# A trunk layer with 32 experts: the order of the last experts' weights, the selection tables and the final store are rearranged

## What is computed

```python
def hier_moe(h, lp):                      # top-1 of 4 groups, top-2 of 8 experts in it
    ...
    for e in range(N_EXPERTS):            # 32 experts, D 1024, D_EXPERT 256
        hid = jax.nn.silu(t @ lp['exp_w_gate'][e]) * (t @ lp['exp_w_up'][e])
        y = y + comb[:, e:e + 1] * (hid @ lp['exp_w_down'][e])
...
x = ln_affine(DEEPNORM_ALPHA * x + g2 * hier_moe(h2, lp), lp['ln2_g'], lp['ln2_b'])
```

## Time and profile before

| | us |
|---|---|
| time, median of 3 (715.06 to 717.89) | 716.77 |
| the profiled execution | 715.41 |
| its span in the trace | 713.7 |
| TensorE matmul busy | 635.1 (89%) |
| VectorE busy | 277.9 (39%) |
| ScalarE busy | 109.6 (15%) |
| GpSimd busy | 113.1 (16%) |

### The profile page before, as it was taken

The page is one execution under the profiler, slowest core; times in us unless marked ns, Lnnn a source line. Parts: engine busy times, 40 slices in busy tenths (PEclk is TensorE's granted clock), DMA queues, the critical chain, the costliest instruction groups (busy, mean ns, idle before and its releaser), DMA issues.

```text
span 713.7 us, 8198 instructions
## 1 busy us (share of the span) xinstructions
PE 635.1 (89%) x3225; PEld 346.4 (49%) x3225; DVE 277.9 (39%) x568; ACT 109.6 (15%) x227; POOL 113.1 (16%) x115
## 2 busy tenths in 40 slices
PE   2899999999999999999999974899998888888894
PEld 0374345554444455556444453566664544544431
DVE  2421543236745445213224766133333222322247
ACT  0020252220012122215010020211111001100000
POOL 3000000020300000000000221433333222231100
PEclk9679999999999999999999985799999999999998
DMA  9977444236430230308968087599999999999852
GB/s 337 368 247 252 161 182 149 87 118 236 141 119 5 113 118 1 118 3 298 370 246 321 29 296 292 190 406 405 406 405 405 407 404 403 400 403 402 353 214 88
DMA packets 67495, 176.60 MB, mean 247 GB/s; under 512 B 10420, under 2 KB 12500, under 8 KB 67456
## 3 DMA queue, kind: packets, MB, share of 16 engines
q1 hardware_dynamic: 50832, 143.56, 52.8%
q10 hardware_dynamic: 10880, 24.21, 9.6%
q0 software_dynamic: 5744, 8.28, 3.3%
HBM read 174.55 MB, written 11.96 MB: 261 GB/s over the span
## 4 chain that ended last, share of the span: by engine, by line
PE 69%; DMA 15%; DVE 6%; SPq 6%; issue 2%; ACT 1%; POOL 1%; DVEq 0%; POOLq 0%
PE bank L1478 24%; PE bank L1733 10%; DMA X<-exp_w_up 9%; PE bank L1650 6%; PE bank L1664 6%; PE bank L1742 5%; DMA W<-exp_w_up 3%; DMA X<-w_ada 3%; SPq L451 3%; PE bank L1430 2%; PE bank L1608 2%; PE bank L1626 2%; PE bank L1531 1%; PE bank L1719 1%; SPq L461 1%
## 5 line engine op out<-in xcount | busy, mean ns | idle before, releaser
L1478 PE MATMUL bank<-W,Y 128*128 128x512 f32 (+1 forms) x432 | 183.0, 577 | 0.0
L1478 PEld LDWEIGHTS bank<-W,Y 128*128 128x128 f32 x432 | 80.9, 192 | 85.2 <-issue 82.6
L1733 PE MATMUL bank<-X,Y 128*64 128x256 f32 x704 | 86.6, 401 | 11.0 <-DMA X<-exp_w_up 10.2
L1733 PEld LDWEIGHTS bank<-X,Y 128*64 128x64 f32 x704 | 55.7, 145 | 48.0 <-DMA X<-exp_w_up 19.3
L630 POOL TENSOR_TENSOR rstd<-ss,cst 128x1 f32<-128x1 f32 (+3 forms) x21 | 22.6, 1074 | 339.2 <-DVE ss L760 339.2
L673 POOL DMA_INDIRECT Y<-h_rows,gidx x32 | 41.4, 1293 | 105.4 <-PE bank L1719 93.9
L1139 DVE COPY abias<-bank 128x128 f32<-128x128 f32 x32 | 9.3, 291 | 122.0 <-PE bank L1764 122.0
L1733 PE MATMUL bank<-W,Y 128*64 128x256 f32 (+1 forms) x320 | 39.7, 368 | 9.0 <-DMA W<-exp_w_up 4.6
L1742 PE MATMUL bank<-X,abias 128*64 128x512 f32 x176 | 42.6, 602 | 1.8 <-issue 1.8
L678 POOL DMA_INDIRECT pair_rows<-PTr,sidx x32 | 32.5, 1014 | 65.8 <-DVE PTr L1153 59.3
L1650 PE MATMUL bank<-W,Y 128*128 128x512 f32 x96 | 42.0, 594 | 0.3 <-PE bank L1650 0.3
(11 more groups left out here) (224 smaller groups left out, 705.6 us busy)
## 6 DMA issues: line engine op xcount, KB each, us to landing
X<-exp_w_gate SPq DMA_DIRECT2D x22, 1024.0 KB
X<-exp_w_up SPq DMA_DIRECT2D x22, 1024.0 KB
X<-exp_w_down SPq DMA_DIRECT2D x22, 1024.0 KB, 19.2
W<-w_in SPq DMA_DIRECT2D x8, 2048.0 KB, 9.0
Y<-w_ada ACTq DMA_DIRECT2D x8, 2048.0 KB, 9.2
W<-exp_w_gate SPq DMA_DIRECT2D x10, 1024.0 KB
W<-exp_w_up SPq DMA_DIRECT2D x5, 1024.0 KB
W<-exp_w_down SPq DMA_DIRECT2D x5, 1024.0 KB
```

Of the source, the lines that this page charges most:

```text
L1478: ins = mm(bank[:, 0:cols], hT[:, i, k, :], w[:, k, :], start=k == 0, stop=k == KT - 1)
L1733: ins = mm(bank[hh * 64:hh * 64 + 64, a:b], x_[:, c, h * 64:h * 64 + 64], rhs(hh), start=k == 0 and a == 0, stop=k == KT - 1, skip_group_c ...
```

## The change

1. SyncE's loop issues down of 29 ahead of gate and up of 30, and down of 30 ahead of gate and up of 31. Down of 31 comes last, as before. Gate and up of 31 get a semaphore each.
2. TensorE runs gate_up of 30 behind down of 29 and gate_up of 31 behind down of 30, the latter first all of gate, then all of up (`last_gate_up`). VectorE's product moves with it.
3. The token numbers, both selection tables and `alphaI` move to constants that are dead by then; SyncE loads them behind gate and up of expert 6, and VectorE builds the tables behind expert 6.
4. The `residual` and `add_rows` matmuls are spread: two `add_rows` of expert 30 stand ahead of hidden of 31, the others go tile by tile.
5. GpSimd adds the pair of tile 2, and TensorE multiplies that tile's `fin` once for each half.
6. The last tile's final operation and its store are halved; the second half is stored from ScalarE's queue.

```diff
 CHECK = 28
+SERIAL = 29
...
             .rearrange("p (j n) -> p j n", n=NE)
-        spare = X[:, 2 * SLOTW:3 * SLOTW]
-        tokr = spare[:, 0:TOKENS]
-        sel = spare[:, TOKENS:(1 + LAST) * TOKENS].rearrange("p (e t) -> p e t", e=LAST)
-        alphaI = spare[:, (1 + LAST) * TOKENS:(1 + LAST) * TOKENS + P]
+        tokr = const("incl_f", 0, TOKENS)
+        sel = [const("excl_b", 0, TOKENS), tokr]
+        alphaI = const("ropeC", 0, P)
         sg, hid, hidT = (abias[:, 0, k * P:(k + 1) * P] for k in range(3))
...
             "settled mod_stored mod_in gate2_in slots_done round_done ada_in weights_asked weights_full "
-            "w_step cleared zeros_y tok_in sel_ready alpha_ready acc_full").split()}
+            "w_step cleared zeros_y tok_in sel_ready alpha_ready acc_full gate_in up_in ctx_added").split()}
         x_in = [sem(f"x_in{i}") for i in range(TILES)]
...
-            for n in range(NBUF, NE + 1):
-                if n < NE:
-                    sp.wait_ge(S["gu_full"], n - NBUF + 1)
+            def refill_down(n):
+                if n >= NBUF:
+                    sp.wait_ge(S["y_full"], n - NBUF + 1)
+                load_down(sp, n, n % NBUF, ed_in[n % NBUF])
+
+            for n in range(NBUF, NE):
+                if n == SERIAL + 1:
+                    refill_down(SERIAL)
+                sp.wait_ge(S["gu_full"], n - NBUF + 1)
+                if n < NE - 1:
                     load_gate_up(sp, n, n % NBUF, ew_in[n % NBUF])
-                m = n - 1
-                if m >= NBUF:
-                    sp.wait_ge(S["y_full"], m - NBUF + 1)
-                load_down(sp, m, m % NBUF, ed_in[m % NBUF])
+                else:
+                    load_part(sp, "exp_w_gate", 0, n, n % NBUF, S["gate_in"])
+                    load_part(sp, "exp_w_up", 1, n, n % NBUF, S["up_in"])
+                if n == NBUF:
+                    sp.dma_start(tokr, T["consts"][:, NCONST:]).then_inc(S["tok_in"], 16)
+                refill_down(n - 1 if n <= SERIAL else n)
...
             overflow(sp, again)
-            sp.wait_ge(S["slots_done"], 1)
-            sp.wait_ge(S["y_full"], CHECK)
-            sp.dma_start(tokr, T["consts"][:, NCONST:]).then_inc(S["tok_in"], 16)
             sp.wait_ge(S["moe_done"], 1)
...
                 sp.wait_ge(S["out_ready"], i + 1)
-                dst = T["o_sample"][0, i * P:(i + 1) * P, :] if i < LAT_TILES else T["o_prompt"][0]
-                sp.dma_start(dst, fin(i, 0)).then_inc(S["out_done"], 16)
-            sp.wait_ge(S["out_done"], 16 * TILES)
+                if i < TILES - 1:
+                    sp.dma_start(T["o_sample"][0, i * P:(i + 1) * P, :], fin(i, 0)).then_inc(S["out_done"], 16)
+                else:
+                    sp.dma_start(T["o_prompt"][0][:, 0:HALF], fin(i, 0)[:, 0:HALF]).then_inc(S["out_done"], 16)
+            sp.wait_ge(S["out_done"], 16 * (TILES + 1))
...
             pool.sem_inc(S["moe_done"], 1)
+            pool.wait_ge(fin_in[CTX], 32)
+            nc.gpsimd.tensor_tensor(fin(CTX, 0), fin(CTX, 0), fin(CTX, 1), ALU.add).then_inc(S["ctx_added"], 1)
             for i in range(TILES):
...
                     overflow(dve, experts)
-                    V.tensor_scalar(alphaI, ident, ALPHA, None, ALU.mult).then_inc(S["alpha_ready"], 1)
                 hidden(n)
-                if n + 1 < NE:
+                if n < SERIAL and n + 1 < NE:
                     gate_times_up(n + 1)
...
                 evict(n)
-                if n == SENT - 1:
+                if n >= SERIAL and n + 1 < NE:
+                    gate_times_up(n + 1)
+                if n == NBUF:
                     dve.wait_ge(S["tok_in"], 16)
                     for e in range(LAST):
-                        ins = V.tensor_scalar(sel[:, e, :], tokr, gf[:, SENT + e:SENT + e + 1], None, ALU.is_equal)
+                        ins = V.tensor_scalar(sel[e], tokr, gf[:, SENT + e:SENT + e + 1], None, ALU.is_equal)
                     ins.then_inc(S["sel_ready"], 1)
+                    V.tensor_scalar(alphaI, ident, ALPHA, None, ALU.mult).then_inc(S["alpha_ready"], 1)
...
                 dve.wait_ge(S["pow_done"], powers[0])
-                tell(V.scalar_tensor_tensor(f, f, rstd[:, 0:1], ln2(1), ALU.mult, ALU.add), "out_ready")
+                if i < TILES - 1:
+                    tell(V.scalar_tensor_tensor(f, f, rstd[:, 0:1], ln2(1), ALU.mult, ALU.add), "out_ready")
+                    continue
+                for h in range(2):
+                    cols = slice(h * HALF, (h + 1) * HALF)
+                    V.scalar_tensor_tensor(f[:, cols], f[:, cols], rstd[:, 0:1], ln2(1)[:, cols], ALU.mult, ALU.add)\
+                        .then_inc(S["out_ready"], 1)
...
                     overflow(act, experts)
+            act.wait_ge(S["out_ready"], TILES + 1)
+            act.dma_start(T["o_prompt"][0][:, HALF:D], fin(CTX, 0)[:, HALF:D]).then_inc(S["out_done"], 16)
...
+            def last_gate_up(bank, x_, w, done):
+                wg, wu = ebuf[w][0]
+                for landed, a, b, wx in ((S["gate_in"], 0, P, wg), (S["up_in"], P, 2 * P, wu)):
+                    pe.wait_ge(landed, 16)
+                    for k in range(KT):
+                        h, c = k // 4, k % 4
+                        for hh in range(2):
+                            ins = mm(bank[hh * 64:hh * 64 + 64, a:b], x_[:, c, h * 64:h * 64 + 64],
+                                     wx[:, k, hh * P:(hh + 1) * P], start=k == 0 and a == 0, stop=k == KT - 1,
+                                     skip_group_check=True)
+                ins.then_inc(done, 1)
+
             def gate_up(bank, x_, w, done):
...
             def next_gate_up(n):
-                pe.wait_ge(ew_in[n % NBUF], (n // NBUF + 1) * 32)
+                if n < NE - 1:
+                    pe.wait_ge(ew_in[n % NBUF], (n // NBUF + 1) * 32)
                 pe.wait_ge(S["xTe_ready"], n + 1)
...
                     pe.wait_ge(S["hid_ready"], n - 1)
-                gate_up(gub[n % 2], xTe[:, n % 2], n % NBUF, S["gu_full"])
+                work = gate_up if n < NE - 1 else last_gate_up
+                work(gub[n % 2], xTe[:, n % 2], n % NBUF, S["gu_full"])
...
                 half = slice(h * SLOT_ROWS, (h + 1) * SLOT_ROWS)
-                return mm(acc[i][h][:, :], sel[half, e, i * P:(i + 1) * P], Yo[half, (SENT + e) % NY, :],
+                return mm(acc[i][h][:, :], sel[e][half, i * P:(i + 1) * P], Yo[half, (SENT + e) % NY, :],
                           start=False, stop=e == LAST - 1, skip_group_check=True)
...
                     pe.nop().then_inc(S["slots_done"], 1)
+                    pe.wait_ge(S["sel_ready"], 1)
                     pe.wait_ge(S["alpha_ready"], 1)
                     residual(0, 1)
-                if n + 1 < NE:
+                if n < SERIAL:
                     next_gate_up(n + 1)
+                if n == NE - 1:
+                    pe.wait_ge(S["y_ready"], NE - 1)
+                    for h in range(2):
+                        add_rows(0, 0, h)
                 hidden(n)
...
                 elif n == SENT + 1:
+                    residual(2, 1)
+                next_down(n)
+                if n >= SERIAL and n + 1 < NE:
+                    next_gate_up(n + 1)
+            for i in range(TILES):
+                if i == TILES - 1:
                     residual(2, 0)
-                next_down(n)
-            residual(2, 1)
-            pe.wait_ge(S["sel_ready"], 1)
-            for i in range(TILES):
-                for h in range(2):
-                    add_rows(0, i, h)
-            for i in range(TILES):
-                pe.wait_ge(fin_in[i], 32)
+                if i:
+                    for h in range(2):
+                        add_rows(0, i, h)
                 if i < TILES - 1:
                     pe.wait_ge(S["added"], i + 1)
+                else:
+                    pe.wait_ge(S["ctx_added"], 1)
                 for h in range(2):
-                    for k in range(1 if i < TILES - 1 else TOPK):
-                        mm(acc[i][h][:, :], ident, fin(i, k)[:, h * HALF:(h + 1) * HALF], start=False, stop=False,
-                           skip_group_check=True)
+                    mm(acc[i][h][:, :], ident, fin(i, 0)[:, h * HALF:(h + 1) * HALF], start=False, stop=False,
+                       skip_group_check=True)
                 if i == 0:
```

## The result

The median of 8 executions is 711.36 us (708.64 to 713.68), beside 715.35 us (713.48 to 717.89) for 8 executions of the kernel before on the same chip. The ratio is 0.9944 (0.9921 to 0.9968), a gain of 4.0 us with an interval from 2.3 to 5.7.

The account below looks back on a forecast made before the run. DMA was taken to bound the expert loop, so only the tail could gain: 3.8 us to bn_stats, plus 0.3 store, less 0.05, less 1.6 for the clock gives 2.45, from 716.77 to 714.3 us; range 711.7 to 716.2.

Parts of the forecast that it names:

- the median is 1.36 above the profiled execution: Base of the sums: before's profiled execution took 715.41 us, its median 716.77; sums were moved by that difference.
- forecast A: Clock falls in TensorE's 2.0 us gap behind down of 31: gain 2.45 us, median 714.3 us, chance 0.47.
- rival B: TensorE's clock stays up through the gap behind down of 31: gain 4.05 us, median 712.7 us, chance 0.35.
- The clock falls: Idle 2.0 us before the identity matmuls drops TensorE to 1.2 GHz, costing about 1.6 us on tile 0's matmuls.
- the store: Halved last operation and store at the end: 0.3 us gained, between 0 and 0.65, less 0.05 for the two halves.
- tile 2: TensorE's 8.8 us for tiles 1 and 2 is even with VectorE's 8.78: cost 0 to 0.3 us, taken as 0.
- The stream: Weight loads at the loop's end: up of 30 at 672.5 us, behind down of 29 (2.6) and token numbers (0.5).
- TensorE and the serial part: From down of 28, 0.8 us earlier, through experts 30 and 31 on TensorE: down of 31 ends at 687.4 us.
- the split by halves: Separate waits for gate and up of 31 in its gate_up: worth nothing but 1 us of margin.
- GpSimd's add: Tile 2's pair add on GpSimd: taken as 2.4 us, hidden up to 3.7 us.
- D: GpSimd's add holds the power VectorE needs; each us above 3.7 is on the path, 721 us at 12; chance 0.06.
- Rival C: Late weights or `fin` replace the removed waits: 1 to 2.5 us go back, median 715.5 us, chance 0.12.

Follow-up runs that it names:

- after_third: The changed kernel, unchanged, run once more: 711.87 us, ratio 0.9955 to the kernel before; loop time (first refill issue to end of span) 255.61 us, with a clock fall.
- after_again: The changed kernel, unchanged, measured again: 711.38 us against 714.28 for the kernel before, ratio 0.9961; loop time 253.96 us, clock up.
- tables_alone: The kernel before with only part 3 (token numbers, tables and `alphaI` early): 714.24 us, ratio 0.9992 to before; loop time 255.73 us.
- one_store: The changed kernel with part 6 undone, last operation and store whole: 712.1 us, ratio 0.9953 to before; loop time 255.49 us, with a clock fall.
- pool_thrice: The changed kernel with GpSimd's add done twice more into a dead buffer ahead of the real one: 712.94 us in one execution, loop time 257.06 us.
- old_order: The changed kernel with the order of parts 1 and 2 undone, split of the last weights kept: 712.63 us, ratio 0.9964 to before; loop time 255.63 us.
- all_rows_first: The changed kernel with all six `add_rows` of expert 30 directly behind down of 31: 712.87 us, ratio 0.9981 to before; loop time 255.44 us.
- pair_on_tensore: The changed kernel with part 5 undone, TensorE multiplying both `fin` of tile 2: 712.95 us, ratio 0.9989 to before; loop time 256.74 us.

## Why the prediction missed

**The base.** The step "the median is 1.36 above the profiled execution" failed. It rested on three executions of before (716.77). With eight the median is 715.35, and in the later comparisons it was 713.93 to 715.14, always below the profiled 715.41. From 715.35, forecast A with its 2.45 us of gain would have been 712.9 and not 714.3, well inside the range, and rival B 711.3; the whole range moved in the same way would be 710.3 to 714.8 and hold the measured time. So 1.4 of the 2.9 us between 714.3 and the measured 711.36 are the base. The spread lies ahead of the loop: over the three profiles of before the first refill moved by 3.8 us, the loop time by 0.1.

**The clock.** This is the other step. "The clock falls" took 1.6 us off the gain. In the profiled execution it did not fall, as in rival B. The step rested on gaps in the DMA-bound stretch of one profile; behind this gap the clock fell in four of nine profiles, and in one of the four of the kernel after itself (`after_third`). So A and B are not two outcomes of which one is right; each holds for a part of the executions. The price of a fall, 1.6 forecast, is 1.65 measured.

That B's 4.05 us of gain and the measured 4.0 agree is partly luck. The same two kernels differed by 2.9 us (`after_again`) and 2.6 us (`after_third`) in the later comparisons, which is nearer to A's 2.45, and the intervals of all three ratios hold the gains of both A and B. The medians can't tell the two apart; the granted clock in the profiles can. Of the 4.08 us between the two profiled executions 0.46 are an earlier start of the loop, which is chance, and 3.6 are in the loop, 0.4 less than B's sum: the store (0.25) and tile 2 (0.15) are most of it.

**The stream.** Up of 30 was forecast at 672.5; its weights are there at 671.8, 672.3 on before's scale of time. Against the refill, up of 30 is there 2.9 us later than before; 2.6 for down of 29 and 0 to 0.2 for the tokens, in place of 0.5, make most of that. (The DMA share is at 9 tenths or more to the 37th slice, 660 us, not to the 38th.)

**TensorE and the serial part.** Down of 28 was to start 0.8 earlier with `alphaI` built long before: 666.58 against 667.97, less the 0.46, is 0.9. Down of 31 was to end at 687.4: it ended at 686.89, which is 687.35 on before's scale. 0.70 us from gate_up to hidden, 1.0 for the residual, 1.94 for each down all held. So did the gap, 2.0 forecast and 1.98 measured. One step does not fit its own numbers: the split by halves was called worth nothing but margin, while gate_up of 31 was to start at 679.8 and its up weights to land at 680.9. From `tables_alone`, up of 31 would land at about 221.6 + 2.6 = 224.2 behind the refill (an estimate), and gate_up of 31 started at 223.5, so without the split some 0.7 us of wait would be left; no run takes the split alone out of the new order. bn_stats was to start at 692.4: 692.03, or 692.5 on before's scale. The gain to this point is 3.7 us against 3.8.

**Tiles, store, GpSimd.** Tile 2 waits 0.15 or 0.16 us in every profile of after, inside the 0 to 0.3, taken as 0. The store was to gain 0.25: beside `one_store` nothing is left of it. The first half is issued 0.64 us before the last operation ends, but the last bytes move only 0.5 us sooner, the two half operations take 0.14 longer than the whole one, and from the last bytes to the end it takes 0.4 longer. GpSimd's add was taken as 2.4: 2.34. The estimate of 2.3 us from the Trainium skill, "GPSIMD Engine Reference", section "Performance versus the Vector engine", agrees with it. D did not come, since the add is short and the scatter of 29 early; `pool_thrice` and `old_order` show it where the add is longer or starts late. Rival C did not come either: no wait took the place of those removed. `old_order` has the waits for `fin` that C feared.

**What the parts are worth.** In loop times: part 3, with the tables, the tokens and `alphaI`, 1.84 of the 3.6 us (`tables_alone`). Taken away from the whole change, the order costs 1.7 (`old_order`, all of it by way of the scatter, `fin` and the power), the spread of the `add_rows` 1.5 (`all_rows_first`), GpSimd's pair 1.7 (`pair_on_tensore`, without what came from upstream), and the halved store nothing. These don't add up to 3.6, since each is worth more with the others in place: with the old order, GpSimd's add is itself on the path.

## What to carry to other kernels

Before a forecast of less than 1% is tied to a median of three, find the point in the trace from which the executions of one kernel agree, and make the sum from there; most of the spread here lay in front of it. A gain at the end of a stream is worth what the last chain allows, so follow each moved step to the queues that start from it: the whole value of the new order was an earlier scatter and what starts from it, two engines on. Where two waits of about the same length run side by side, as the tokens and `alphaI` did, one profile shows only the one that ended last. An idle stretch of TensorE on the path can have a price beyond its length, and other work put into it (here a VectorE add moved to where VectorE stood idle) removed both.

## What the runs showed of the chip

- A gap of 1.98 us in front of the same matmuls was followed by 2.4 GHz in some executions and by 1.2 GHz in others, 4 of 9 for gaps of 1.98 to 2.10 us; behind 3.12 us it fell in the one profile. A gap of 1.90 us in the kernel before was followed by a fall in two profiles of three.
- A VectorE operation with two SBUF inputs took 2.71 instead of 1.28 us beside a GpSimd add of 2.33 us that had begun before it.
- Two stores of 256 KB on two queues landed in 2.0 us each and moved their last bytes 0.5 us sooner behind the last VectorE operation than one of 512 KB (2.6 us), and the program still ended no sooner.
